# Attention's work in an extra buffer and half the ring, the first gate weights loaded and rounded during it, both layers written out

## The chip, the cores and the metric

The kernel runs on one core of a Trainium2 chip. Its engines are TensorE (PE, matrix products; PEld is its loading of weights), VectorE (DVE), ScalarE (ACT), GpSimd (POOL) and SyncE (SP), whose queue issues nearly all transfers between the chip's memory (DRAM) and the on-chip memory (SBUF). Products land in PSUM (`ps`, 8 banks of 512 floats per partition). The metric is the device time of one execution, in microseconds.

## The reference, cut to what matters

Two layers of one block, and then a second block that the change touches only in how one buffer is handed over. Of each of the two layers this matters (512 tokens, width 1024, fp32):

```python
def _mixer(h, w_in, qn_g, kn_g, w_pa, w_pb, w_o, cos, sin, slopes):
    proj = h @ w_in
    qa, ka, va, qd, kd, vd, gates = jnp.split(proj, IN_SPLITS, axis=-1)
    ...
    out_a = _global_gqa(qa, ka, va)                  # 8 heads, 2 key heads
    ...                                              # 12 dilated heads in 3 groups
    out_b = jnp.sum(wts[..., None] * jnp.stack(outs, 0), 0).reshape(b, s, B_OUT)
    g_a, g_b = jnp.split(jax.nn.sigmoid(gates), 2, axis=-1)
    merged = g_a * (out_a @ w_pa) + g_b * (out_b @ w_pb)
    return merged @ w_o
```

Behind the mixer each layer has a layer norm, a mixture of 16 experts and a second layer norm. `mod = silu(c) @ w_ada + b_ada` gives shifts, scales and gates for the norms.

## The kernel before, in words

**Products in three parts.** Every fp32 weight is cut into a rounded high part (`w_hi`) and a low part (`w_lo`), and so are the activations (`hT_hi`, `hT_lo`). A product is high*high + high*low + low*high. Raw weights arrive in `ring`, two halves of 128 x 2048 floats (1 MB each). For half `i` of unit `u`: SyncE loads `ring[i]` (L121, once the low part before is done), ScalarE rounds it into `w_hi[i]` (L132), VectorE subtracts to get `w_lo[i]` (L144), and TensorE multiplies (L283), first everything that needs `w_hi`, then what needs `w_lo`. The class `Weights` holds the semaphores.

**Stages.** A layer is a row of stages, each a block of five instruction streams with a barrier of all engines behind it: `norm_to_hT`, `in_projection`, `attention`, `branches`, `norm_to_hT`, `moe`, `norm_to_hT`. The two layers run in a hardware loop (L2495), so each engine has a jump back behind layer 1, and addresses that depend on the layer are computed in registers.

**attention** (L1570). 48 groups: 32 "global" ones (one head, 128 queries, 512 keys), then 16 "dilated" ones. For group `i`, TensorE multiplies queries and keys (L1618), VectorE takes the maximum (L1712), ScalarE the exponential into `pr` (L1670), TensorE transposes it (L1641), ScalarE (odd global groups and all dilated ones, L1691) or VectorE (even global ones, L1752) copies the result out of PSUM into `pT`, TensorE multiplies it with the values (L84), and VectorE scales the result (L1740). In each round `i` ScalarE does the exponential of group `i`, then the copy of group `i-1` if it is its own. Three buffers `pr`, three `sc` and two `pT` (512 floats each) take turns; before, all eight lie in the ring, which nothing else uses in this stage. Beside it SyncE issues, in this order and each line waiting for the one before: the two bias tables and 11.8 MB of zeros into a table in DRAM that the experts use later (`slots_x`); `v0c` out to DRAM; `v0` back in another order (three transfers). All of that is L1605, and L1611 is the last wait.

**branches** (L1758). Its first four units are the gate weights (TensorE's half units of 32 + 16 products), then the two branches and the output. SyncE: both halves of unit 0, `U0` out to DRAM (L1808), the modulation sums (`tmp_b`, `braw`, `gates`, rows), then `U0` back in another order (L1814), three pieces of `w_ada` (L1034), the halves of unit 1, more pieces. TensorE: 32 small products (`warm_up`, L102), half unit (0, 0), then the sums over rows (L1096, L1101, L1868), a wait for the modulation (`tail.mod_done`), then half unit (0, 1) and all others. VectorE: the low parts of both halves, a wait for `U0`, the weights of the three groups (L1933 to L1936), four quarter pieces (L1048, L1054), the end of the modulation (`tail.finish`, L1117), which TensorE waits for.

`k.ahead` are two semaphores, one for each half of the ring, that count loads issued in the stage before the one that uses them; they are never cleared, so the waits name totals (16 a load).

## Time and profile before

| | us |
|---|---|
| median of 3 runs | 3522.6 (3502.38 to 3526.61) |
| profiled execution | 3511.61 |
| its span in the profile | 3509.8 |
| PE busy | 3075.4 (88%) |
| DVE busy | 2230.2 (64%) |
| ACT busy | 1220.9 (35%) |
| POOL busy | 391.8 (11%) |
| attention, layer 1 and 2 | from 214.3 and from 1059.0, some 97 us each |
| branches, layer 1 and 2 | from 312.3 and from 1156.9 |

The page shows the engines' busy time, but an average over 3.5 ms says little of two places of some 100 us. The timeline (each instruction or run of equal ones with its start, its duration, and in brackets the idle time ahead of it and what ended that) is read around these places, the windows give the granted TensorE clock and the DMA engines' share in a stretch, and the waits say what a queue waited for. `SPq` are instructions of SyncE's queue.

### The profile page before, as it was taken

What the parts mean: (1) busy time and instruction counts of PE and PEld (TensorE: products, weight loads), DVE (VectorE), ACT (ScalarE), POOL (GpSimd) and SP (SyncE); (2) the same over time, 40 slices, a digit from 0 to 9 for tenths busy, and PEclk for the clock granted to TensorE, in tenths of its full rate; (3) what the DMA queues carried; (4) which work ended last, traced back from release to release, by engine and by line L of the source; (5) the groups of instructions that cost most, each with busy time, mean ns of one, the idle gap of its engine ahead of it and who ended that gap; (6) DMA issues with size and microseconds to landing.
All of it is one profiled execution on the core that took longest, in us unless ns stands there. A gap on an engine that the chain in (4) does not pass through costs nothing. (4 is left out here: it accounts for less than half of the span.)

```text
span 3509.8 us, 39676 instructions
## 1 busy us (share of the span) xinstructions
PE 3075.4 (88%) x14763; PEld 2487.9 (71%) x14763; DVE 2230.2 (64%) x3130; ACT 1220.9 (35%) x1629; POOL 391.8 (11%) x152
## 2 busy tenths in 40 slices
PE   4998977996799896899499799789999898889999
PEld 3777866774677784877377578668887687758887
DVE  6765575997666567699643747666664565464445
ACT  2234223764325333466222725431111222341112
POOL 0000001000000000100000000304443000014443
PEclk9999987998899997899699999989999899989999
DMA  7754535997645642799552033124442352112222
GB/s 249 250 177 151 192 103 182 367 403 274 221 162 175 208 159 86 275 403 395 196 191 84 25 125 100 41 83 156 143 144 69 128 174 97 60 48 95 93 93 80
DMA packets 285298, 583.87 MB, mean 166 GB/s; under 512 B 21562, under 2 KB 129538, under 8 KB 278077
## 3 DMA queue, kind: packets, MB, share of 16 engines
q1 hardware_dynamic: 272744, 537.87, 44.3%
q10 hardware_dynamic: 7764, 26.85, 1.9%
q0 software_dynamic: 4608, 16.78, 1.3%
q8 instruction: 109, 1.79, 0.2%
q14 instruction: 73, 0.59, 0.1%
HBM read 529.46 MB, written 78.71 MB: 173 GB/s over the span
## 5 line engine op out<-in xcount | busy, mean ns | idle before, releaser
L132 ACT CAST w_hi<-ring 128x2048 fp32r<-128x2048 f32 (+2 forms) x166 | 308.8, 1863 | 1212.5 <-PE ps L283 1021.8
L283 PE MATMUL ps<-hT_hi,w_hi 128*128 128x512 f32 (+1 forms) x1256 | 503.3, 401 | 25.2 <-DVEq L1117 11.3
L283 PE MATMUL ps<-hT_lo,w_hi 128*128 128x512 f32 (+1 forms) x1256 | 500.5, 399 | 0.0
L139 POOL TENSOR_TENSOR w_lo<-ring,w_hi 128x2048 fp32r<-128x2048 f32 x64 | 307.3, 4803 | 906.6 <-ACTq L2931 521.3
L144 DVE TENSOR_TENSOR w_lo<-ring,w_hi 128x2048 fp32r<-128x2048 f32 (+3 forms) x112 | 245.4, 2195 | 229.4 <-ACT w_hi L132 229.1
L283 PE MATMUL ps<-hT_hi,w_lo 128*128 128x512 f32 (+1 forms) x1256 | 307.9, 397 | 9.9 <-DVE w_lo L144 9.9
L283 PEld LDWEIGHTS ps<-hT_hi,w_hi 128*128 128x128 f32 (+1 forms) x1256 | 240.1, 191 | 86.1 <-DVEq L1117 13.0
L283 PEld LDWEIGHTS ps<-hT_hi,w_lo 128*128 128x128 f32 (+1 forms) x1256 | 237.8, 190 | 67.5 <-DVE w_lo L144 11.6
L283 PEld LDWEIGHTS ps<-hT_lo,w_hi 128*128 128x128 f32 (+1 forms) x1256 | 239.9, 191 | 56.0
L1054 DVE SCALAR_TENSOR_TENSOR piece_sums<-pieces,cond,piece_sums 128x512 f32<-128x512 f32 x294 | 220.8, 751 | 92.6 <-DMA pieces<-in_w_ada_dram 57.8
L283 PE MATMUL ps<-w_hi,hT_hi 128*128 128x512 f32 (+1 forms) x672 | 259.9, 389 | 1.0 <-ACT w_hi L132 1.0
L283 PE MATMUL ps<-w_hi,hT_lo 128*128 128x512 f32 (+1 forms) x672 | 259.0, 387 | 0.0
L283 PE MATMUL ps<-w_hi,hid_hi 128*128 128x512 f32 x448 | 174.4, 389 | 0.0
L283 PE MATMUL ps<-w_hi,hid_lo 128*128 128x512 f32 x448 | 174.4, 389 | 0.0
L2996 DVE TENSOR_TENSOR hid_exact<-hid_exact 128x512 f32<-128x512 f32 x64 | 162.1, 2532 | 4.0 <-DVE hid_exact L2993 0.6
L283 PE MATMUL ps<-w_lo,hT_hi 128*128 128x512 f32 (+1 forms) x672 | 158.2, 387 | 0.0
L283 PEld LDWEIGHTS ps<-w_hi,hT_hi 128*128 128x128 f32 x672 | 126.4, 188 | 28.6 <-issue 1.8
L283 PEld LDWEIGHTS ps<-w_hi,hT_lo 128*128 128x128 f32 x672 | 126.4, 188 | 26.8
L283 PEld LDWEIGHTS ps<-w_lo,hT_hi 128*128 128x128 f32 x672 | 124.2, 188 | 27.4 <-DVE w_lo L144 0.3
L102 PE MATMUL ps<-ident_sb 128*128 128x128 f32 x696 | 100.9, 317 | 48.6 <-PEq L72 48.6
L102 PEld LDWEIGHTS ps<-ident_sb 128*128 128x128 f32 x696 | 98.7, 231 | 51.9 <-issue 51.9
L3015 DVE TENSOR_TENSOR y<-y,ps 128x512 f32<-128x512 f32 x48 | 33.0, 688 | 157.1 <-PE ps L283 155.8
(596 smaller groups left out, 5929.6 us busy)
## 6 DMA issues: line engine op xcount, KB each, us to landing
ring<-in_mlp_w_dram SPq DMA_DIRECT2D x64, 1024.0 KB, 5.2
pieces<-in_w_ada_dram SPq DMA_DIRECT2D x96, 512.0 KB, 5.9
ring<-in_w_in_dram SPq DMA_DIRECT2D x36, 1024.0 KB, 6.5
pieces<-in_mod_w_dram SPq DMA_DIRECT2D x72, 512.0 KB, 5.1
raw_sep<-in_w_exp_gate_dram SPq DMA_DIRECT2D x50, 512.0 KB
raw_sep<-in_w_exp_up_dram SPq DMA_DIRECT2D x50, 512.0 KB
raw_sep<-in_w_exp_down_dram SPq DMA_DIRECT2D x24, 1024.0 KB
ring<-in_e_w_in_dram SPq DMA_DIRECT2D x24, 1024.0 KB, 5.6
```

What stands on the lines that cost most here:

```text
L102: pe.matmul(k.ps[:, bank, 0:P], k.ident[:], k.ident[:], start=True, stop=True)
L132: self.k.nc.scalar.copy(self.k.parts[0][:, i, 0:words], self.k.ring[:, i, 0:words]).then_inc(self.high, 1)
L139: self.k.nc.gpsimd.tensor_tensor(self.k.parts[1][:, i, 0:words], self.k.ring[:, i, 0:words], self.k.parts[0][:, i, 0:words].bitcast(F32), ...
L144: self.k.nc.vector.tensor_tensor(self.k.parts[1][:, i, 0:words], self.k.ring[:, i, 0:words], self.k.parts[0][:, i, 0:words].bitcast(F32), ...
L283: mm = pe.matmul(out, a if weight_left else b, b if weight_left else a, start=first and part == 0 and q == ks[0] and o == 0, stop=last and ...
L1054: ins = V.scalar_tensor_tensor(acc, slot[:, q, :], f, acc, ALU.mult, ALU.add)
L2996: link(V.tensor_tensor(e, e, e, ALU.mult))
L3015: link(V.tensor_tensor(yv, yv, k.ps[:, 4 * b + t, :], ALU.add))
```

## The change

- In the first block attention's eight buffers are split: `pr` and one `pT` lie in half 1 of the ring, `sc` and the other `pT` in a new buffer `work` (128 x 2048 floats). Half 0 of the ring is free.
- SyncE, behind the last of its loads in attention, loads the first half of the first gate weights into `ring[0]`.
- ScalarE, in round 24 of 48, between the exponential of group 24 and the copy of group 23, waits for that load and rounds it into `w_hi[0]`.
- In `branches` SyncE loads only half 1 of unit 0, ScalarE rounds only half 1, and TensorE's 32 warm-up products are gone.
- The loop over the layers is a Python loop: both layers are written out, and the totals of `k.ahead` become constants.
- The window attention of the second block gets its eight buffers as two fours of the same buffer.

```diff
-def attention(k, groups, loads=(), space=None, late=(), ahead=None, warm=12):
+def attention(k, groups, loads=(), space=None, late=(), ahead=None, warm=12, round_at=None):
...
-        idle = k.ring[:].rearrange("p b n -> p (b n)").rearrange("p (a n) -> p a n", a=8) if space is None else space
-        pr, sc, pT = idle[:, 0:3], idle[:, 3:6], idle[:, 6:8]
+        pr, sc, pT = space[0][:, 0:3], space[1][:, 0:3], (space[0][:, 3], space[1][:, 3])
...
             if ahead is not None:
                 k.load_ahead(sp, ahead)
+                if len(ahead) == 1:
+                    sp.nop().then_inc(k.ahead[1], 16)
...
             for i in range(N + 1):
                 if i < N:
                     soften(i)
+                if round_at is not None and i == N // 2:
+                    act.wait_ge(k.ahead[0], round_at)
+                    nc.scalar.copy(k.parts[0][:, 0, :], k.ring[:, 0, :])
                 v = i - 1
...
-            weights(0, 0)
+            sp.wait_ge(k.ahead[0], ahead)
+            sp.nop().then_inc(W.landed[0], 16)
             weights(0, 1)
...
-            split(0, 0)
+            act.nop().then_inc(W.high, 1)
             split(0, 1)
...
         def _(pe):
-            W.start_read(pe)
+            pe.nop().then_inc(W.read, 2)
+
...
+                    work = b.enter_context(nc.sbuf_tensor(fresh("work"), [P, 4, 512], F32))
...
+                              space=(k.ring[:, 1, :].rearrange("p (a n) -> p a n", a=4), work[:]),
+                              ahead=k.first_halves(kp(A["w_in"]), C_GATE, feature=True)[0:1], round_at=32 * l + 32)
...
-    with k.nc.Fori(0, DEPTH) as l:
+    for l in range(DEPTH):
         first_layer(k, l, mid)
```

ScalarE's stream in attention, at rounds 23 to 26. `L1670` before is `L1671` after, `L1691` is `L1695`; `ring` and `work` are where the buffers lie. Before:

```order
L1670 ACTIVATE ring,ls<-ps,neg_max 128x512 x2
L1691 COPY ring<-ps 128x512
L1670 ACTIVATE ring,ls<-ps,neg_max 128x512 x2
L1691 COPY ring<-ps 128x512
L1670 ACTIVATE ring,ls<-ps,neg_max 128x512 x2
```

After:

```order
L1671 ACTIVATE ring,ls<-ps,neg_max 128x512 x2
L1689 CAST w_hi<-ring 128x2048
L1695 COPY work<-ps 128x512
L1671 ACTIVATE ring,ls<-ps,neg_max 128x512 x2
L1695 COPY work<-ps 128x512
L1671 ACTIVATE ring,ls<-ps,neg_max 128x512 x2
```

The cast stands between the second exponential of a pair (group 24) and the copy of group 23.

SyncE's stream from the attention of a layer into `branches` (a branch instruction opens each stage). Before:

```order
L1605 DMA slots_x<-const_zeros_dram 128x23x1024
L1605 DMA scratch<-v0c 128x1040
L1605 DMA v_40<-scratch 128x3x260
L1605 DMA v_40<-scratch 64x260 x2
L68 UNCONDITIONAL_BRANCH
L1793 UNCONDITIONAL_BRANCH
L121 ISA
L121 DMA ring<-in_w_in_dram 128x8x256
L121 ISA
L121 DMA ring<-in_w_in_dram 128x8x256
L1808 DMA scratch<-U_98 128x4x264
```

After:

```order
L1604 DMA slots_x<-const_zeros_dram 128x23x1024
L1604 DMA scratch<-v0c 128x1040
L1604 DMA v_40<-scratch 128x3x260
L1604 DMA v_40<-scratch 64x260 x2
L264 DMA ring<-in_w_in_dram 128x8x256
L68 UNCONDITIONAL_BRANCH
L1797 UNCONDITIONAL_BRANCH
L121 DMA ring<-in_w_in_dram 128x8x256
L1813 DMA scratch<-U_98 128x4x264
```

One of the two ring loads has moved from the head of `branches` to the end of attention's list, and the register arithmetic (`ISA`) ahead of the loads is gone.

## Rows read from the trace of the kernel before

**Rows 1.** The page's first part: busy time, share of the span, instructions.
```profile
PE 3075.4 (88%) x14763; PEld 2487.9 (71%) x14763; DVE 2230.2 (64%) x3130; ACT 1220.9 (35%) x1629; POOL 391.8 (11%) x152
```

**Rows 2.** Timeline, ScalarE, attention, both layers: start, duration, what [idle before, releaser].
```profile
261.99 0.69 ACT L1670 ACTIVATE ring<-ps,neg_max 128x512 f32<-128x512 f32 x1 [0.69 <-DVE neg_max L1712]
...
263.80 0.59 ACT L1691 COPY ring<-ps 128x512 f32<-128x512 f32 x1 [1.03 <-PE ps L1641]
...
265.75 0.69 ACT L1670 ACTIVATE ring<-ps,neg_max 128x512 f32<-128x512 f32 x1 [0.69 <-DVE neg_max L1712]
...
1108.51 0.59 ACT L1691 COPY ring<-ps 128x512 f32<-128x512 f32 x1 [1.03 <-PE ps L1641]
```

**Rows 3.** Timeline, SyncE's queue, attention of layer 1.
```profile
215.19 0.71 SPq L1605 DMA_DIRECT2D slots_x<-const_zeros_dram  x1
...
265.56 1.57 SPq L1605 DMA_DIRECT2D v<-scratch  x3
```

**Rows 4.** Waits of SyncE's queue, attention of layer 1: total, times, longest.
```profile
SPq L1605 <- DMA slots_x<-const_zeros_dram: 47.0, 1, 47.0
```

**Rows 5.** Line L1611: duration in ns, first and last start (layers 1 and 2).
```profile
L1611 SPq EVENT_SEMAPHORE  x2: 17/17/17, 270.9 to 1115.5; - x2
```

**Rows 6.** Timeline, TensorE, start of branches in layer 1.
```profile
312.31 5.44 PE L102 MATMUL ps<-ident_sb 128*128 128x128 f32 x32 [1.61 <-PEq L72]
319.98 0.79 PE L283 MATMUL ps<-hT_hi,w_hi 128*128 128x512 f32 x1 [2.23 <-ACT w_hi L132]
...
340.74 1.02 PE L1868 MATMUL ps<-gates,ones_b 128*128 128x512 f32 x2
347.34 0.80 PE L283 MATMUL ps<-hT_hi,w_hi 128*128 128x512 f32 x1 [5.58 <-DVEq L1117]
```

**Rows 7.** Timeline, VectorE, the same stretch.
```profile
332.69 0.18 DVE L1933 TENSOR_TENSOR Mx<-U,U 128x16 f32<-128x16 f32 x1 [6.29 <-DMA U<-scratch]
...
345.19 1.54 DVE L1054 SCALAR_TENSOR_TENSOR piece_sums<-pieces,cond,piece_sums 128x512 f32<-128x512 f32 x2 [6.58 <-DMA pieces<-in_w_ada_dram]
```

**Rows 8.** Windows: stretch, length, busy by engine (count), PEclk, DMA share, GB/s.
```profile
314.00:333.00 19.00, 16.77 (x74) 13.95 (x73) 4.86 (x4) 3.80 (x2) 0.00 (x0) 0.85 1.01 369
323.40:341.80 18.40, 18.36 (x82) 13.05 (x80) 7.29 (x12) 1.63 (x2) 0.00 (x0) 0.91 1.05 384
347.30:350.70 3.40, 3.36 (x8) 2.68 (x9) 3.32 (x3) 0.00 (x0) 0.00 (x0) 0.52 0.49 154
400.00:440.00 40.00, 40.00 (x190) 33.45 (x189) 20.38 (x26) 11.35 (x16) 0.00 (x0) 1.00 0.52 169
279.00:310.50 31.50, 30.56 (x279) 27.94 (x278) 24.63 (x49) 20.07 (x41) 7.34 (x7) 1.00 0.01 1
3051.50:3061.70 10.20, 10.12 (x64) 8.86 (x64) 6.52 (x21) 5.84 (x22) 0.00 (x0) 0.71 0.01 2
```

**Rows 9.** Timeline, VectorE, first instruction behind layer 1 and behind layer 2.
```profile
888.38 0.69 DVE L1215 BATCH_NORM_STATS2 stats<-x_res 128x6 f32<-128x512 f32 x1 [4.99 <-issue]
...
1733.71 0.06 DVE L1105 MEMSET ones_m<- 128x1 f32 x1 [1.24 <-PEq L72]
```

**Rows 10.** Line L1670 up to 262.8 and up to 1107.5: count, ns, first and last start.
```profile
L1670 ACT ACTIVATE ring<-ps,neg_max x25: 682/690/696, 219.1 to 262.0; 128x512 f32<-128x512 f32 x25
...
L1670 ACT ACTIVATE ring<-ps,neg_max x25: 680/689/696, 1063.8 to 1106.7; 128x512 f32<-128x512 f32 x25
```

**Rows 11.** Gate load issued at 364.50 in branches: us from issue to landing.
```profile
DMA to landing us min/median/max: 5.1/5.1/5.1
```

**Rows 12.** Timeline, ScalarE, the first rounding in branches of layer 1.
```profile
318.02 1.90 ACT L132 CAST w_hi<-ring 128x2048 fp32r<-128x2048 f32 x1 [8.52 <-DMA ring<-in_w_in_dram]
```

**Rows 13.** Timeline, TensorE, window attention of the second block.
```profile
3051.58 2.08 PE L1618 MATMUL ps<-skT,sqT 64*128 64x256 f32 x8 [1.06 <-ACT attention_space L1680]
...
3058.07 1.14 PE L1618 MATMUL ps<-skT,sqT 64*128 64x256 f32 x8
...
3062.62 1.13 PE L1618 MATMUL ps<-skT,sqT 64*128 64x256 f32 x8 [0.70 <-ACT attention_space L1680]
```

More of the change, by code:

```diff
@@ L249, in __init__ @@
         self.ahead = [c.enter_context(nc.semaphore(n)) for n in ("ahead0_landed", "ahead1_landed")]
-        self.ahead_n = 16 * DEPTH
+        self.ahead_n = 32 * DEPTH
         self.bias_moved = c.enter_context(nc.semaphore("bias_moved"))
@@ L1357, in _, with in_projection @@
                         router.logits(pe, out, q)
-def in_projection(k, w, hT, T, gq, gk, w_side, side_out, ahead):
+def in_projection(k, w, hT, T, gq, gk, w_side, side_out, ahead, x_moves):
     nc = k.nc
@@ L1408, in _ @@
             sp.wait_ge(in_landed, 48)
-            sp.wait_ge(k.x_moved, 4 * ahead)
+            sp.wait_ge(k.x_moved, x_moves)
             side.end(sp, 8)
@@ L1651, in _ @@
                         n, w = vs[0].shape[-1], width(v)
-                        mm = chain(pe, k.ps[:, 4 + v % 2, h * n:(h + 1) * n], lambda j: pT[:, v % 2, h * w + j * P:h * w + (j + 1) * P],
+                        mm = chain(pe, k.ps[:, 4 + v % 2, h * n:(h + 1) * n], lambda j: pT[v % 2][:, h * w + j * P:h * w + (j + 1) * P],
                                    lambda j: vs[j], range(len(vs)))
@@ L1690, in _ @@
                         act.wait_ge(o_ready, v - 1)
-                    nc.scalar.copy(pT[:, v % 2], k.ps[:, 2 + v % 2, :]).then_inc(t_act, 1)
+                    nc.scalar.copy(pT[v % 2], k.ps[:, 2 + v % 2, :]).then_inc(t_act, 1)
         @block.gpsimd
@@ L1751, in _ @@
                         dve.wait_ge(o_ready, v - 1)
-                    V.tensor_copy(pT[:, v % 2], k.ps[:, 2 + v % 2, :]).then_inc(t_dve, 1)
+                    V.tensor_copy(pT[v % 2], k.ps[:, 2 + v % 2, :]).then_inc(t_dve, 1)
                 if i >= 2:
@@ L1755, in _, with branches @@
             dve.wait_ge(o_out, N)
-def branches(k, w_in, wa, wb, wo, hT, T, tail_of, sums, b, g1, g2, w_side):
+def branches(k, w_in, wa, wb, wo, hT, T, tail_of, sums, b, g1, g2, ahead, w_side):
     nc = k.nc
@@ L2427, in first_layer @@
                 in_projection(k, kp(A["w_in"]), hT, T, A["q_norm_g"][l], A["k_norm_g"][l],
-                              lambda s: ada[0][:, :, 2 * D + s * WIDE:2 * D + (s + 1) * WIDE], lambda s: sums[:, s * WIDE:(s + 1) * WIDE], 16 * l + 16)
+                              lambda s: ada[0][:, :, 2 * D + s * WIDE:2 * D + (s + 1) * WIDE], lambda s: sums[:, s * WIDE:(s + 1) * WIDE], 32 * l + 16, 64 * l + 64)
                 T["oa"] = T["qa"]
@@ L2435, in first_layer @@
                               loads=[[(band[:], k.K["bias_band"]), (cls[:], k.K["bias_class"]),
-                                      (k.slots_x.rearrange("(b p) d -> p b d", p=P), bcast(k.K["zeros"], 1, BLOCKS))]] + order_v0(k, T["v0c"], T["v0"]))
+                                      (k.slots_x.rearrange("(b p) d -> p b d", p=P), bcast(k.K["zeros"], 1, BLOCKS))]] + order_v0(k, T["v0c"], T["v0"]),
+                              space=(k.ring[:, 1, :].rearrange("p (a n) -> p a n", a=4), work[:]),
+                              ahead=k.first_halves(kp(A["w_in"]), C_GATE, feature=True)[0:1], round_at=32 * l + 32)
             first = k.sums_2[0].rearrange("p (l n) -> l p n", l=2)[l]
@@ L2441, in first_layer @@
             branches(k, kp(A["w_in"]), kp(A["w_branch_a"]), kp(A["w_branch_b"]), kp(A["w_out"]), hT, T,
-                     (sums[:, D:3 * D], A["b_ada"][l][3 * D:5 * D], 16, k.mod[:, 24:40], (8,), None), sums, A["b_ada"][l][2 * D:6 * D], g1, g2,
+                     (sums[:, D:3 * D], A["b_ada"][l][3 * D:5 * D], 16, k.mod[:, 24:40], (8,), None), sums, A["b_ada"][l][2 * D:6 * D], g1, g2, 32 * l + 32,
                      (lambda s: 0 if s < n_next else 1, lambda s: at(ada[1], s) if s < n_next else at(w_first, s - n_next),
@@ L3660, in odd_mixer @@
             ring = lambda i: k.ring[:, i, :].rearrange("p (k n) -> p k n", k=4)
-            attention(k, groups, warm=28, space=space, late=moves, ahead=[(ring(i), wo[:, KD:KD + 4, 512 * i:512 * (i + 1)]) for i in range(2)])
+            attention(k, groups, warm=28, space=(space[:, 0:4], space[:, 4:8]), late=moves, ahead=[(ring(i), wo[:, KD:KD + 4, 512 * i:512 * (i + 1)]) for i in range(2)])
             hT = pair_of(nc, h, "hT", [P, KD, S], side="right")
```

## Prediction, made before the change was timed

> **What bounds the kernel now.** The page comes first: TensorE is busy for 88% of the span [rows 1], so time is won where it stands still or runs at its lower clock. The change touches three such places: the attention and the start of the stage behind it (`branches`), each once per layer, and the edge between the two layers. I read the timeline of each, engine by engine.
>
> *Attention.* The groups go round in a steady beat, two groups in 3.77 us (exponential 24 starts at 261.99 and 26 at 265.75 [rows 2]). TensorE has no idle time in it, and ScalarE has two short gaps in a beat: 1.03 us ahead of the copy of the transposed weights, which waits for TensorE's transposes, and 0.69 us ahead of every second exponential, which waits for VectorE's maximum. What matters for the change is SyncE's queue beside it [rows 3]: it issues a transfer of 11,776 KB of zeros at 215.19 and waits 47.0 us for it [rows 4]; the reordering of `v0` then takes two dependent steps more (the second is issued at 265.56), and the last wait ends at 270.9 in layer 1 and at 1115.5 in layer 2 [rows 5].
>
> *Start of `branches`.* The first product is at 319.98, though TensorE entered the stage at 312.31: it waits for the load and the rounding of half 0 [rows 6]. Half 0 and the sums behind it end at 341.76 (340.74 plus 1.02). Then TensorE stands still for 5.58 us, and the second half unit starts at 347.34. What ends last there is not a weight but VectorE, which must first work on four quarter pieces and finish the modulation sums. Its own waits end on transfers: `U` at 332.69 and the fourth piece at 345.19 [rows 7]. From 314 to 333 the DMA engines' share is 1.01, and from 323.4 to 341.8 it is 1.05 [rows 8]. So the second half unit, behind which TensorE is busy nearly all the time (40.00 of 40 us from 400 to 440 [rows 8]), is held by the bytes queued on SyncE's queue. Layer 2 looks the same.
>
> *Edge of the layers.* VectorE's first instruction of layer 2 starts at 888.38, after 4.99 us of idle time that nothing but issue explains. At the end of layer 2, out of the same stage but with no jump back, it is 1.24 us [rows 9].
>
> **The change part by part.**
>
> 1. *The wait inside attention.* ScalarE's new rounding stands behind exponential 24 and ahead of the copy for group 23, as the order shows. It waits for the load of the first gate half, which SyncE issues behind everything of [rows 3 to 5]. Exponential 24 is the 25th of its kind: 25 have started by 262.0 and by 1106.7 [rows 10]. Layer 1: the issue at 270.95; landing after 5.1 us, as the same form of load took on a quiet queue [rows 11], with 0.1 for the slower of the others in that stage, so 5.2; landed 276.15. The rounding is 1.90 us (the same cast at 318.02 [rows 12]): done 278.05. The copy that it pushes stood at 263.80, so 14.25 us late. Layer 2: 1115.55 + 5.2 + 1.90 = 1122.65 against 1108.51 [rows 2], 14.14 us late. Queued behind the waiting instruction on ScalarE are all later exponentials and copies; TensorE needs the copy for its next value product and exponential 25 for its next transposes, VectorE needs those products for its results. Nothing else feeds them, so all stop within a beat. Work done meanwhile is one maximum and one copy on VectorE; at the restart that saves the 0.69 us wait, once. Sum: 28.4 - 1.4 = +27.0 us.
>
> 2. *TensorE's clock after that stop.* TensorE stands still for about 13 us. After the 5.58 us stop at 341.8 the granted clock was 0.52 for the next 3.4 us [rows 8], the lower of the two levels (1.2 GHz). What an attention beat costs there is shown by the window attention of the second block: from 3051.58 to 3058.07, most of it at the low clock (mean 0.71 from 3051.5 to 3061.7 [rows 8]), a pair of groups took 6.49 us, and 4.55 us from there to 3062.62 at the full one [rows 13]. That is 1.9 us for a pair. Bounds: nothing, and two such pairs, 3.9 us. I take one, 1.9 us a layer: +3.8 us.
>
> 3. *The 1 MB load leaves `branches`.* SyncE's list there loses its first transfer and keeps its order. TensorE then starts products at once, some 7.6 us earlier (319.98 - 312.31), and the half unit and its sums are done some 7 us earlier. But the next half unit waits for the modulation, and that for the fourth piece. Its bytes stand in one queue with one load fewer: 1.05 MB at 384 GB/s (the row for 323.4 to 341.8 [rows 8]) is 2.7 us. The removed issue lies in this time. Bounds: nothing if latency and not bytes sets the chain; 7.6 us if the pieces are no bound. A share of 1 is that of a full queue, so 2.7 us: -5.4 us for both layers.
>
> 4. *The 32 warm-up products go.* They lay ahead of the first product and end with it; in that half unit even a cold start is hidden, since TensorE has over ten microseconds to wait behind it. Eight products at 0.43 us (3.40 us for 8 [rows 8]) in place of 0.21 (40 us for 190) would cost 1.8 us there and reach nobody. If that cover were gone it would be 1.8 us a layer. Nothing.
>
> 5. *Both layers written out.* The jump back goes: 4.99 - 1.24 = 3.75 us. SyncE loses register arithmetic ahead of its issues; in both stages above it waits for others or for bytes, so I count nothing for that. Sum: -3.75 us.
>
> 6. *The extra buffer and half the ring* have the same shapes and the same rotation of three and two, so no wait is added. Nothing. The window attention gets the same space cut in two: nothing.
>
> Sum: 27.0 + 3.8 - 5.4 - 3.75 = **+21.7 us**. On the profiled execution, 3511.6 us with a span of 3509.8, that is 3533 us. The median of the runs shown, 3522.6, would give 3544. The profiled one lies between the runs (3502.38 to 3526.61), so I say 3538 us. Between -35 and +35 us lies what a measurement of this kernel cannot tell from no change (1%), and my forecast is inside it.
>
> **The rivals.**
>
> *B: the start of `branches` is worth all of the 7.6 us.* For it: TensorE's idle time ahead of the first product names ScalarE's rounding. Against it: the 5.58 us stop behind it. Time: 27.0 + 3.8 - 15.2 - 3.75 = +11.9, so 3528 us.
>
> *C, the other side: ScalarE does not stop.* Were the first gate half there by 262.8, the rounding would fill the 1.03 us gap and cost 0.87 us more a layer, and the sum is 1.7 - 5.4 - 3.75 = -7.4, so 3509 us. That needs the zeros' transfer to be some 13.4 us shorter than its 47.0 us, or the wait not to hold. It decides where the copy comes 4.6 us late in each layer, half of the gains' 9.15 us. Against it: SyncE's last wait ends 8.9 us behind exponential 24 in layer 1 and 8.8 us in layer 2 [rows 5, 10], so the place is steady, and nothing that the change moves stands ahead of it.
>
> *D: the clock stays low for the rest of attention.* From 279 to 310.5 TensorE is busy for 30.56 of 31.50 us at clock 1.00 [rows 8], so at half clock it would need up to twice that: up to +30 us a layer, 3538 + 56 = 3594 us at the most, and 3566 us if half of the stretch is low. Against it: the window attention came back to 1.00 after two pairs [rows 13].
> The Trainium skill has a rule for D: "TensorE: Matmul & The Clock Gate", section "HAM oscillation — how this bites in real kernels", says that small gaps between groups of products can let the clock swing between its levels. The trace of attention does not agree: 1.00 through the whole stage. By the rule the sum would be D's, by the row it is mine.
>
> **How the numbers follow.** Forecast 0.72, B 0.12, C 0.05, D 0.11. The range takes in B and the runs' own scatter below, and half of D's lower case above: 3510 to 3566 us. Faster by over 1% needs a case that I don't have: 0.02. Slower by over 1% is D and the upper end of the forecast (second pair at the low clock, a median like the 3526 run): 0.18. The rest, 0.80, lies within 1%.
>
> **What would show it.** Right: in each layer a single ScalarE idle time of about 13.5 us ahead of the new cast, ended by the load of the ring; SyncE's last wait in attention still near 271; attention longer by 15 to 17 us; the first product of `branches` right at the stage's entry, but the second half unit only some 2.7 us earlier in its stage; VectorE's gap between the layers 1.2 us. Wrong: the cast starts within 2 us of exponential 24 (C); the second half unit follows the first without a stop (B); the granted clock at 0.5 for over 10 us behind the restart (D).

## The result and the profile after

The changed kernel takes 3525.3 us (median of 22 runs, 3517.9 to 3538.7), the kernel before beside it 3518.5 us (22 runs): ratio 1.0023, 95% interval 1.0012 to 1.0034, that is 8 us more (4 to 12). I had said 21.7 us more. The time lies in my range and within the 1%, but the change of the time was forecast nearly three times too large, and it will show that this came from errors of opposite sign, of which the largest is in step 5.

Three places carry the result. First ScalarE and SyncE in attention of both layers (timeline: start, duration, what, idle before and who ended it; the SPq rows are SyncE's issues), to be held against [rows 2, 3]:

```profile
261.31 0.69 ACT L1671 ACTIVATE ring<-ps,neg_max 128x512 f32<-128x512 f32 x1 [0.69 <-DVE neg_max L1716]
...
271.62 1.90 ACT L1689 CAST w_hi<-ring 128x2048 fp32r<-128x2048 f32 x1 [9.53 <-DMA ring<-in_w_in_dram]
273.42 0.58 ACT L1695 COPY work<-ps 128x512 f32<-128x512 f32 x1
...
1121.24 0.69 ACT L1671 ACTIVATE ring<-ps,neg_max 128x512 f32<-128x512 f32 x1 [0.69 <-DVE neg_max L1716]
...
1132.91 1.90 ACT L1689 CAST w_hi<-ring 128x2048 fp32r<-128x2048 f32 x1 [10.89 <-DMA ring<-in_w_in_dram]
1134.72 0.58 ACT L1695 COPY work<-ps 128x512 f32<-128x512 f32 x1
```

```profile
262.68 1.56 SPq L1604 DMA_DIRECT2D v<-scratch  x3
266.48 0.39 SPq L264 DMA_DIRECT2D ring<-in_w_in_dram  x1
```

Exponential 24 starts at 261.31, and the cast waits 9.53 us in layer 1 and 10.89 us in layer 2 for the load of the ring, just the one idle time that the prediction named, though 4.0 and 2.6 us shorter than its 13.5 us. The copy used to follow the exponential by 1.81 us (263.80 against 261.99 [rows 2]); now it follows by 12.11 and by 13.48, so it is 10.3 and 11.7 us late.

TensorE behind the stop of layer 1, as timeline and as windows (length, busy time of each engine, granted clock, DMA share, GB/s), the last three windows those of layer 2:

```profile
263.76 0.61 PE L1642 MATMUL ps<-ident_sb,ring 128*128 128x128 f32 x4
274.05 1.97 PE L84 MATMUL ps<-kva,work 128*128 128x64 f32 x8 [9.68 <-ACT work L1695]
275.95 2.08 PE L1619 MATMUL ps<-kaT,qaT 64*128 64x512 f32 x4
...
283.06 2.08 PE L1619 MATMUL ps<-kaT,qaT 64*128 64x512 f32 x4
```

```profile
274.00:301.60 27.60, 27.55 (x124) 23.02 (x125) 10.49 (x26) 8.46 (x21) 2.10 (x2) 0.50 0.00 1
303.00:312.40 9.40, 9.33 (x93) 8.38 (x93) 8.49 (x18) 5.89 (x12) 2.10 (x2) 1.00 0.00 1
312.40:331.00 18.60, 18.45 (x165) 16.96 (x164) 13.84 (x27) 12.21 (x25) 4.20 (x4) 1.00 0.00 1
1135.30:1141.50 6.20, 6.15 (x24) 4.53 (x25) 1.05 (x3) 2.44 (x7) 0.00 (x0) 0.52 0.00 0
1141.50:1149.00 7.50, 7.50 (x69) 6.49 (x69) 5.19 (x14) 3.51 (x11) 0.00 (x0) 1.00 0.00 0
1149.00:1172.00 23.00, 22.12 (x207) 19.93 (x206) 19.35 (x40) 13.28 (x29) 6.29 (x6) 1.00 0.01 2
```

In layer 1 of this execution the granted clock is 0.50 (the level of 1.2 GHz) when TensorE goes on, a beat takes 7.11 us (from 275.95 to 283.06) in place of 3.77, and the clock is back only at some 301.6, after 27.6 us in which TensorE was busy for 27.55 us and did half of what it does at the full clock. In layer 2 it is back after some 6 us, though the stop ahead of it was longer. The first of these is what the prediction gave as a sign of rival D: 0.5 for over 10 us behind the restart.

Start of `branches` in layer 1, TensorE and then VectorE, against [rows 6, 7]:

```profile
333.32 0.47 PE L283 MATMUL ps<-hT_hi,w_hi 128*128 128x512 f32 x1 [1.47 <-ACTq L1839]
333.63 0.39 PE L283 MATMUL ps<-hT_lo,w_hi 128*128 128x512 f32 x1
333.86 0.40 PE L283 MATMUL ps<-hT_hi,w_hi 128*128 128x512 f32 x1
...
363.65 0.80 PE L283 MATMUL ps<-hT_hi,w_hi 128*128 128x512 f32 x1 [9.46 <-DVEq L1117]
```

```profile
350.05 0.19 DVE L1939 TENSOR_TENSOR Mx<-U,U 128x16 f32<-128x16 f32 x1 [6.20 <-DMA U<-scratch]
...
361.50 1.54 DVE L1054 SCALAR_TENSOR_TENSOR piece_sums<-pieces,cond,piece_sums 128x512 f32<-128x512 f32 x2 [5.52 <-DMA pieces<-in_w_ada_dram]
```

Products begin at the stage's entry. The stop ahead of the second half unit is still there, for the same pieces, and grew from 5.58 to 9.46 us. That half unit starts 30.3 us behind the entry (363.65 - 333.32) in place of 35.0 (347.34 - 312.31 [rows 6]), and the pieces still end what VectorE waits for.

The edge of the layers, against 4.99 in [rows 9]:

```profile
903.98 0.69 DVE L1215 BATCH_NORM_STATS2 stats<-x_res 128x6 f32<-128x512 f32 x1 [1.02 <-PEq L72]
```

The page's first part, against [rows 1], names no bound that moved: the products are fewer by the 64 warm-ups, and the time longer.

```profile
span 3532.6 us, 38936 instructions
...
PE 3079.9 (87%) x14699; PEld 2489.7 (70%) x14699; DVE 2231.5 (63%) x3130; ACT 1217.6 (34%) x1628; POOL 391.3 (11%) x152
```

### The profile page after: what moved, and what is told of

The parts are those of the page before. It is cut to its first block and busy times, and to the rows that moved or that the text cites. A ratio compares the mean times of both kernels' runs of the same rounds, so it can differ in the third digit from the quotient of the medians.

```text
span 3532.6 us, 38936 instructions
## 1 busy us (share of the span) xinstructions
PE 3079.9 (87%) x14699; PEld 2489.7 (70%) x14699; DVE 2231.5 (63%) x3130; ACT 1217.6 (34%) x1628; POOL 391.3 (11%) x152
## 5 line engine op out<-in xcount | busy, mean ns | idle before, releaser
L283 PEld LDWEIGHTS ps<-hT_hi,w_lo 128*128 128x128 f32 (+1 forms) x1256 | 235.8, 188 | 65.8 <-DVE w_lo L144 10.7
```

The lines of the kernel that those rows point to most:

```text
L283: mm = pe.matmul(out, a if weight_left else b, b if weight_left else a, start=first and part == 0 and q == ks[0] and o == 0, stop=last and ...
```

## The experiments

A table first. Medians; "clock" is the mean granted clock over all runs of a kernel (the kernel before: 0.9284 over 88 runs). Ratios are to runs of the kernel before on the same chip in the same job, whose medians were 3518.9 (the first four rows), 3514.6 (buffers split and 72 calls), 3516.6 (the next four), 3519.7 (4 writes) and 3518.2 (1 and 8 writes).

| kernel | us (runs) | ratio, 95% interval | clock |
|---|---|---|---|
| the change again | 3526.5 (12) | 1.0038 [1.0017, 1.0059] | 0.9254 |
| only written out | 3497.1 (6) | 0.9938 [0.9923, 0.9954] | 0.9327 |
| change, load issued first | 3495.5 (6) | 0.9940 [0.9926, 0.9955] | 0.9317 |
| change, rounding in round 32 | 3505.2 (5) | 0.9958 [0.9946, 0.9971] | 0.9294 |
| written out, buffers split | 3493.5 (6) | 0.9932 [0.9916, 0.9948] | 0.9323 |
| change, 72 warm-up calls in the stop | 3530.5 (10) | 1.0039 [1.0022, 1.0056] | 0.9326 |
| two loops of one pass | 3496.5 (8) | 0.994 [0.9922, 0.9959] | 0.9336 |
| change with the loop | 3539.7 (5) | 1.0067 [1.0039, 1.0095] | 0.9242 |
| change, 40 warm-up calls in the stop | 3527.1 (10) | 1.0036 [1.0016, 1.0056] | 0.9286 |
| change, load first and round 32 | 3499.0 (10) | 0.9962 [0.9945, 0.998] | 0.9295 |
| two loops, 4 writes between | 3510.3 (10) | 0.9977 [0.9962, 0.9992] | 0.9308 |
| two loops, 1 write between | 3502.1 (10) | 0.9955 [0.9937, 0.9973] | 0.9327 |
| two loops, 8 writes between | 3515.1 (10) | 0.9992 [0.9977, 1.0007] | 0.9307 |

**The change again.**

> The changed kernel once more, beside the others of this job. The runs gave a ratio of 1.0023 to the kernel before, and the single profiled execution was 22.8 us longer in span. Theory A (the stop of ScalarE costs about 10.4 us a layer, the start of branches gives back 4.4, the edge of the layers 4, TensorE's clock adds an amount that differs from execution to execution): ratio 1.002 to 1.004. Rival (the profiled pair is typical): 1.006.

Measured: the casts start at 270.27 and 1115.61, behind 8.55 and 10.39 us of idle time, and the low clock behind the stop of layer 1 is over sooner: the beats are back at 3.77 us from 279.62 on. The long stretch at the low clock is thus no fixed cost, but it is one that comes. The three profiles with a stop (these two and that of the change with the loop, below) hold six stops of TensorE, of 8.7 to 11.0 us. Read by the transposes behind them (four take 1.1 us at the low clock and 0.6 us at the full one), the low clock lasted some 28, 6, 4, 6, 13 and 6 us, and the longest stretch did not follow the longest stop.

**Only the writing out.** The kernel before with `for l in range(DEPTH)` in place of the loop over the layers.

> The kernel before with both layers written out and nothing else. The edge of the layers should lose its 4.99 us of issue time for about 1.1 us. Theory A: -4 us, ratio 0.9989, and both attentions as before (98 us each). Rival (writing out does nothing, or costs elsewhere in fetching code): ratio 1.000 or above.

Measured: 0.9938, some 22 us less where the theory had 4 and the rival none. This is the surprise of the case: at the edge only 4 us are gained.

**The stop taken away in two ways.** The load issued ahead of the bias tables and the zeros:

```diff
             n = 0
+            if ahead is not None and loads:
+                k.load_ahead(sp, ahead)
+                sp.nop().then_inc(k.ahead[1], 16)
             for pairs in loads:
```

> The changed kernel, but SyncE issues the ring's load ahead of the bias tables and the zeros in attention, so that it has landed long before round 24. Theory A: ScalarE doesn't stop, the new rounding costs up to 0.9 us a layer, attention is 98 to 100 us long, and against the kernel before the time is -4 (edge) - 9 (branches) + 2 = -11 us, ratio 0.997. Rival 1 (the stop is not what costs, but the split buffers or the rounding itself are): ratio stays at 1.002. Rival 2 (TensorE's clock falls in attention for another reason): attention stays above 105 us.

and the wait with its rounding put to the first dilated group (32), which waits for SyncE's loads anyway:

```diff
             for i in range(N + 1):
-                if i < N:
-                    soften(i)
-                if round_at is not None and i == N // 2:
+                if round_at is not None and i == first_bias:
                     act.wait_ge(k.ahead[0], round_at)
                     nc.scalar.copy(k.parts[0][:, 0, :], k.ring[:, 0, :])
+                if i < N:
+                    soften(i)
```

> The changed kernel, but the wait and the rounding stand at the head of round 32, ahead of the first dilated exponential, where ScalarE waited 2.53 us for GpSimd in the kernel before. The load lands 10.3 us behind exponential 24 in the changed kernel, round 32 is 14 us behind it. Theory A: no stop, the rounding lies in the gap, attention 98 us, ratio 0.9965 (-12 us). Rival (the rounding pushes the first dilated groups by its 1.9 us): -8 us, 0.9977.

Measured: 0.9940 and 0.9958. The timeline of ScalarE in the first of them:

```profile
258.89 0.19 ACT L1672 ACTIVATION_READ_ACCUMULATOR ring<-ps,neg_max 128x1 f32 x1
258.99 1.89 ACT L1690 CAST w_hi<-ring 128x2048 fp32r<-128x2048 f32 x1
260.77 0.58 ACT L1696 COPY work<-ps 128x512 f32<-128x512 f32 x1
```

The same cast in the same round with nothing to wait for: 31 us less than the change (3526.5 - 3495.5, same job). So the stop, with all that it brings behind it, costs the change about 31 us, give or take some 10 by the intervals of the two ratios, and my +27.0 and +3.8 were 30.8.

**The kernel before, two further profiles.**

> The kernel before, profiled once more. Its profiled execution of 3511.6 us is 7 us under the median of 22 runs, and writing out the loop alone brought 22 us where the edge of the layers shows 4. Theory A (the rest is a place that is slow in most executions with the loop, but not in the profiled one): a stage whose length differs by 5 us or more from the profile that I have. Rival (scatter spread over all stages by TensorE's clock): no stage differs by more than 3 us.

> The kernel before, a third profile, for the same question: under theory A the same stage is long again, under the rival other stages are.

Measured: 3501.7 and 3521.9 us, clocks 0.934 and 0.929. One kernel's profiles are 20 us apart, so stages are compared below as means over several.

**Written out, buffers split, nothing else.**

> The kernel before with both layers written out and attention's buffers split between half 1 of the ring and the new buffer; no load or rounding in attention, and branches as before. My step 6 says that the split costs nothing: ratio 0.994, as with the writing out alone. Rival (the place of the buffers matters): off by more than 0.002.

Measured: 0.9932 against 0.9938 without the split: the buffers cost nothing, as step 6 said.

**Keeping TensorE busy in the stop.** First 72 calls of the warm-up product, then 40:

```diff
                     v = i - 2
+                    if round_at is not None and v == N // 2 - 1:
+                        pe.wait_ge(o_out, v - 1)
+                        warm_up(k, pe, 4 + v % 2, 72)
                     moved_out(pe, v)
```

> The changed kernel with 72 small products on TensorE in the stop (about 8.6 us at the full clock), so that its clock does not fall while ScalarE waits. They lie behind the last product that it can do and end before the copy that it waits for. Theory: a stop of 10.4 us a layer stays, what the clock costs behind it (12.8 and 3.5 us in the two layers of the profile) goes: 10 to 15 us faster than the changed kernel, ratio 0.999. Rival (the clock costs little in most executions): ratio 1.003 as the changed kernel.

> The changed kernel with 40 calls of the warm-up product (80 products as the profile counts them, at 0.113 us each some 9.0 us) while TensorE stands still in attention, about 9.7 us in each layer. They end ahead of the stop's end, so that the stop is no longer than in the change; the 72 calls of the experiment before took 16.2 us and made it 5.6 us longer. Theory A, the low clock behind the stop costs a good part: the granted clock is 1.00 behind the stop, attention is 3 to 10 us a layer shorter than in the change, 3510 to 3520 us, ratio 0.998 to 1.001. Theory B, the clock costs my 1.9 us a layer: 3522 us. If the stop of itself were the smaller part, attention plus projection would fall from 259 to 269 us to under 255.

The timeline of TensorE with 72 calls (a call stands as two products), then with 40, and a window behind each:

```profile
261.11 16.24 PE L102 MATMUL ps<-ident_sb 128*128 128x128 f32 x144
277.19 1.00 PE L84 MATMUL ps<-kva,work 128*128 128x64 f32 x8
```

```profile
277.00:312.00 35.00, 34.12 (x309) 29.97 (x307) 26.27 (x58) 18.36 (x40) 6.29 (x6) 1.00 0.00 1
```

```profile
263.09 9.10 PE L102 MATMUL ps<-ident_sb 128*128 128x128 f32 x80
272.02 1.00 PE L84 MATMUL ps<-kva,work 128*128 128x64 f32 x8
272.96 1.13 PE L1619 MATMUL ps<-kaT,qaT 64*128 64x512 f32 x4
...
276.73 1.13 PE L1619 MATMUL ps<-kaT,qaT 64*128 64x512 f32 x4
```

```profile
280.00:287.00 7.00, 7.00 (x68) 6.32 (x67) 5.69 (x14) 2.96 (x7) 1.05 (x1) 1.00 0.01 2
287.00:312.00 25.00, 24.13 (x225) 21.81 (x223) 20.42 (x41) 14.84 (x32) 7.33 (x7) 1.00 0.01 2
```

With 72 calls the products outran the stop, which ScalarE would have ended at 272.2 (its copy starts at 271.63), so that experiment doesn't separate the two costs; it shows only that the clock is 1.00 for the rest of attention when TensorE hadn't stood still. With 40 calls the stop has nearly its own length (in layer 1 they end about 1 us later than ScalarE's copy would have let TensorE go on), and the beat is 3.77 us at once (272.96 to 276.73). Projection plus attention is 255.4 and 257.0 us in the two layers; what the two parts cost follows with the profiles of the kernels with and without a stop (table below). But the timed runs don't follow that profile, which is one of the two quickest of ten (3506 and 3508, the other eight 3520 to 3538): the median is no less than that of the change, 3527.1. That theory A's stage came true and its total did not stays open.

**Is it the jump or the register?** The kernel before with one loop of one pass for each layer:

```diff
-    with k.nc.Fori(0, DEPTH) as l:
-        first_layer(k, l, mid)
+    for at in range(DEPTH):
+        with k.nc.Fori(at, at + 1) as l:
+            first_layer(k, l, mid)
```

> The kernel before, with its one loop over the two layers made two loops of one pass each. Every engine still works out its addresses from the layer's register, but no engine jumps back between the layers, and each layer has its own instructions. Writing out both layers gave 0.9938 [0.9923, 0.9954], some -21.8 us, of which only 4 us stood at the edge. Theory A, the gain comes from the jump back and the instructions behind it being fetched anew: 3497 +- 4 us, ratio 0.994, the edge 18.9 us in place of 22.9. Theory B, it comes from the layer's register (arithmetic and waits ahead of transfers and instructions, all through both layers): ratio 0.999, -4 us, all at the edge. A share in between is told by the stages of the two layers.

Measured: 0.994, all of the gain. But the kernel is not what the expectation says. The first lines of the pages of the kernel before, of the two loops and of the kernel only written out:

```profile
span 3509.8 us, 39676 instructions
```

```profile
span 3492.5 us, 39092 instructions
```

```profile
span 3502.7 us, 39062 instructions
```

With loops of one pass nearly all the work on addresses (FUSED_REGOPS and MOVE, instructions on registers) is gone as well. At L121 the kernel before has these, and the two loops have neither:

```profile
L121 SPq FUSED_REGOPS  x64: 37/37/56, 70.0 to 1321.9; - x64
L121 SPq MOVE ring<-in_w_in_dram x40: 29/29/38, 70.1 to 1231.3; - x40
```

Over the whole trace SyncE's queue has 278 FUSED_REGOPS and 417 MOVE before, 42 and 74 with the two loops, 42 and 72 written out. So this experiment takes the jump back and the register arithmetic away together, as writing out does, and **can't tell one from the other**. It shows that the gain comes again in a second form. VectorE behind the edge:

```profile
886.28 0.17 DVE L1114 TENSOR_TENSOR mod<-ps,bcol 128x16 f32<-128x16 f32 x1
887.74 0.69 DVE L1215 BATCH_NORM_STATS2 stats<-x_res 128x6 f32<-128x512 f32 x1 [1.28 <-PEq L72]
```

1.28 us of idle time for 4.99. One more trace of the loop lies in the page's two queues of instructions: 109 and 73 packets before, 106 and 63 with the two loops and written out.

**The change with the loop put back.**

> The change without its writing out: the loop over the layers is put back into the changed kernel, all else stays. Theory A, writing out is worth some 21 us here too: 3526 + 21 = 3547 us, ratio 1.0085. Theory B, my step 5 (only the jump back): 3526 + 4 = 3530 us, ratio 1.003.

Measured: 3539.7 us, 1.0067, where 1.0023 and 1.0038 were measured written out. Here writing out is worth 10 to 16 us, between the two theories.

**Load first and round 32.**

> The changed kernel with the first gate half loaded ahead of the bias tables and zeros (issued near 213, landed long before it is wanted), and the wait and the rounding at the first group behind the dilated tables' wait. Either alone gave 0.9940 and 0.9958. If the rounding between exponential 24 and its copy costs 0.9 us a layer, as the gap of 1.03 us says, this one stands 1 to 2 us below the early load alone: 3493 us, ratio 0.9935. If the rounding costs nothing anywhere, or the load beside the zeros costs what it saves, it is the same as the early load: 3495 us.

Measured: 0.9962, not faster than either alone. The two don't add up, and no version with the load moved out of `branches` beats the ones that are only written out (0.9938, 0.9932, 0.994).

**Does it matter when the work falls?** Two loops of one pass (so without the register arithmetic) with writes of zeros by VectorE between the layers, four, then one and eight:

```diff
+        if at:
+            with k.nc.sbuf_tensor(fresh("pause"), [P, 4, 1024], F32) as pause, k.nc.Block() as block:
+                @block.vector
+                def _(dve):
+                    for _i in range(4):
+                        k.nc.vector.memset(pause[:, _i], 0.0)
```

> The two loops of one pass again, with four writes of 128x1024 zeros by VectorE between the layers (2 to 5 us with the stage around them), so that the edge is about as long as with the jump back and all work behind it begins about when it did in the kernel before. Theory A1, the jump back costs 4 us at the edge and something else all through the second layer and behind it: this kernel keeps all but those 4 us, 3496 + 4 = 3500 us, mean granted clock 0.933. Theory A2, only the time by which the rest is shifted matters to the low-clock stretches behind it: it is back near 3513 us or above, mean granted clock 0.928 to 0.929 as in the kernel before.

> Two loops of one pass with one write of zeros between the layers in place of four: the added stage is the same, the shift is about 1.7 us in place of 4.9. Four writes gave 3510.3 us, 13.8 more than none, 4.9 of them at the edge. If the 8.9 us beyond the shift come from when the work behind the edge falls (theory A2), one write costs its 1.7 us and some part between 0 and 9 us, and the mean clock says which. If they come from having any stage more there, it is 3496.5 + 1.7 + 8.9 = 3507 us, and the eight writes behind it show the same 8.9.

> The same with eight writes of zeros, a shift of about 9.2 us. Theory A2 (when the work falls): 9.2 us and anything from 0 to some 20 us, with a mean clock between 0.928 and 0.934 that goes with it. A loss of 8.9 us that any added stage brings: 3496.5 + 9.2 + 8.9 = 3514.6 us, mean clock 0.931 as with four writes.

VectorE between the layers with four writes:

```profile
886.44 0.17 DVE L1114 TENSOR_TENSOR mod<-ps,bcol 128x16 f32<-128x16 f32 x1
888.07 0.91 DVE L2501 MEMSET pause<- 128x1024 f32 x1 [1.46 <-PEq L72]
...
892.58 0.69 DVE L1215 BATCH_NORM_STATS2 stats<-x_res 128x6 f32<-128x512 f32 x1 [0.37 <-PEq L2497]
```

From the modulation's last instruction to the layer's first are 6.14 us here and 1.46 us with no write, a shift of 4.7 us. With one write it is 1.5 us and with eight 9.0 us by the same rows. Against 3496.5 us with none:

| writes | shift at the edge | longer by | beyond the shift | mean clock |
|---|---|---|---|---|
| 0 | 0 | 0 | 0 | 0.9336 |
| 1 | 1.5 | 5.6 | 4.1 | 0.9327 |
| 4 | 4.7 | 13.8 | 9.1 | 0.9308 |
| 8 | 9.0 | 18.6 | 9.6 | 0.9307 |

Four writes came out between the two theories (3510.3 us, clock 0.931). One write should have cost 3507 us if any added stage brought the 8.9 us; it has 3502.1 (ten runs, none above 3504.9). These rows come from three jobs; by the ratios to the kernel before the three are longer by 5, 13 and 18 us, each give or take some 8 us, so what one write costs beyond its shift is not clear of noise. Within one job, eight writes are 13.0 us longer than one (3515.1 - 3502.1; the ten runs of each leave 8 to 17) for 7.5 us more at the edge. So time put between the layers costs more than its own length, by the medians up to 9 us more, and the clock of the runs falls with it.

**Where does the clock go?** More profiles of the kernel before and of the two loops.

> The kernel before, one more profile. The runs of the kernel before fall around mean clocks of 0.927 and 0.933, the longer ones at 0.927; profiles so far had 0.932, 0.934 and 0.929, and the one at 0.929 had 34 us more at the low clock between 2365 and 3090 us of the second block, and was 12 us longer there. If the gain of writing out that single profiles don't show (some 10 of the 21 us) is that stretch, a profile of this kernel at 0.925 to 0.929 has it in the second block: some 788 us in place of 771 to 777 us for that part. If it is lost in the second layer, the part stays at 774 and branches and moe of layer 2 are longer than 200 and 315 us.

> The kernel before, a further profile for the same question: of the runs of this kernel about three in four lie at a mean clock of 0.929 or less, so about three in four profiles should have the 788 us part in the second block, if that is where the clock goes.

> The two loops of one pass, a second profile: all eight runs had a mean clock of 0.931 to 0.935. If the second block's part is what tells the two kernels apart, it is 774 us here and the span is 3490 to 3497 us; if it is 785 to 788 us at such a clock, the second block isn't where they differ.

Measured: 3512.5, 3511.8 and 3497.0 us at 0.931, 0.929 and 0.932. The second block's part (from VectorE's first work behind 2365 us to its first at 3146 us) is 776.7 us in both profiles of the kernel before: at 0.929 I had expected 788. That theory falls. The part from 2365 to 3090 us does come in two lengths, but in kernels of the same gain. The windows of it, first the two loops, then the kernel only written out:

```profile
2365.00:3090.00 725.00, 681.83 (x3099) 548.29 (x3099) 434.02 (x604) 173.14 (x236) 143.81 (x30) 0.96 0.36 117
```

```profile
2365.00:3090.00 725.00, 685.81 (x3066) 552.19 (x3064) 432.41 (x601) 171.85 (x234) 143.89 (x30) 0.94 0.35 115
```

Clock 0.96 against 0.94, the part 774 against 785 us, and their medians are the same.

**Stages, as means over profiles.** A stage is counted from VectorE's first instruction in it to the first in the next (the second block from its first layer norm statistics). "Before" are its five profiles, "written out" four (only written out, buffers split, two loops twice), "no stop" three (load first, round 32, both), "stop" three (the change twice, and with the loop), "40 calls" one.

| us | before | written out | no stop | stop | 40 calls |
|---|---|---|---|---|---|
| projection and attention 1 | 247.4 | 246.4 | 246.3 | 264.3 | 255.4 |
| branches 1 | 198.8 | 198.2 | 194.9 | 194.8 | 196.7 |
| moe 1 | 314.3 | 315.5 | 312.9 | 314.4 | 315.0 |
| last norm of layer 1, with the edge | 22.8 | 19.0 | 18.9 | 20.1 | 18.9 |
| projection and attention 2 | 247.5 | 246.9 | 247.3 | 259.6 | 257.0 |
| branches 2 | 199.5 | 198.5 | 197.7 | 195.8 | 197.2 |
| moe 2 | 315.7 | 312.2 | 313.5 | 313.9 | 309.4 |
| second block | 1770.3 | 1769.1 | 1767.3 | 1771.9 | 1762.2 |
| VectorE's last instruction at | 3506.5 | 3495.8 | 3489.0 | 3524.9 | 3501.0 |

## Why the prediction was wrong

**Step 1, the wait: right in kind, too long by a fifth.** ScalarE stops once in each layer behind exponential 24, for the ring's load. The copy is 10.3 and 11.7 us late, 22.0 in all, where the sum had 27.0. The landing was right: 5.14 us (266.48 to 271.62) and 5.22 us in layer 2, forecast 5.2. The issue was not. I took it at the end of SyncE's last wait, 270.9 [rows 5], 5.4 us behind the issue of the last reordering [rows 3]; it is 3.80 us behind it (262.68 to 266.48), and that reordering itself stood 1.4 us behind exponential 24 in place of 3.6. Why those transfers were done sooner no run shows.

**Step 2, the clock: right in kind, too small.** The stage with the stop is 262.0 us on the mean of both layers (264.3 and 259.6), 256.2 with TensorE kept busy, and 246.8 without a stop: 9.4 us a layer for the standing still, 5.8 us for the clock, where I had 1.9. The 256.2 is a single profile, but the low stretches agree with it: half of the six (28, 6, 4, 6, 13 and 6 us) is some 5 us a layer. Two things were too small in my 1.9 us. A beat of attention at the low clock costs 3.3 us more (7.11 - 3.77), not 1.9: the pair in [rows 13] ended at the full clock, and the one that I took off it has 0.70 us of idle time. And the low clock can last far longer than a beat. The errors of steps 1 and 2 cancel: 15.2 us a layer, forecast 15.4. Rival D's mechanism is thus real, and its sign came in two of six stops (28 and 13 us at 0.50), but not to the end of attention each time. The rows against D in the prediction came from a stretch that had had no such stop ahead of it (1.06 us of idle time in [rows 13] and 2.81 us just before), which was no fair witness.

The Trainium skill, "TensorE: Matmul & The Clock Gate", section "HAM oscillation — how this bites in real kernels", says that a wait between groups of products throws the clock back and that each such group then starts cold. (It speaks of waits longer than a group's own products. Small gaps, of which the prediction speaks, stand in the page's next section, "A second HAM failure mode: psum-queue depth-cycling".) The traces agree for the one long wait: 0.50 behind 9.68 us of idle time, and 1.00 where products filled it. That the clock stayed low for 27.6 us in which TensorE stood still for only 0.05 us is more than the section says.

**Step 3, the start of `branches`: right in its stage, absent in the total.** 3.9 us in layer 1 and 1.8 to 3.7 us in layer 2 by the table (198.8 to 194.9; 199.5 to 197.7 and 195.8), forecast 2.7 each; the second half unit comes 4.7 us earlier in its stage in layer 1. The row behind my rate, 384 GB/s, was that of a full queue, but the removed load moved at the stage's entry, where the queue was only filling. This window of the trace of before, which I had not read, gives 226 GB/s, and 1.05 MB at that is 4.6 us, an estimate:

```profile
312.30:318.00 5.70, 5.44 (x32) 5.25 (x32) 0.08 (x2) 0.00 (x0) 0.00 (x0) 0.70 0.76 226
```

Rival B falls: the stop ahead of the second half unit is there, and longer. But the kernels without a stop are not faster in timed runs than those only written out (3495.5, 3505.2, 3499.0 against 3497.1, 3493.5, 3496.5), and their mean clock is lower (0.930 against 0.933). The 4 us by which `branches` is shorter than in those (198.2 to 194.9, 198.5 to 197.7) are not in the medians, which scatter by as much; where they go was not found.

**Step 4, the warm-ups: right.** The first half unit runs at a product each 0.23 us from the start (333.63 to 333.86), with nothing cold to hide, since TensorE comes out of attention at clock 1.00.

**Step 5, writing out both layers: this step failed.** I read the edge, 4.99 - 1.24 = 3.75 us, priced the jump back by that alone, and put SyncE's register arithmetic at nothing because its queue waits in the two stages that I had read. The edge is right, 3.8 us in the table. The whole is 22 us (0.9938, 0.9932, 0.994), and 10 to 16 us in the changed kernel. The term was thus three to six times too small; what makes up the rest is open. What the runs showed in its place:
- The jump back and the register arithmetic are both gone in every kernel that gains, in the two loops of one pass too, and no run has one without the other. The stages speak for what lies at and behind the edge: before it, in layer 1, projection, attention, `branches` and `moe` are 760.5 us before and 760.1 us written out, in layer 2 they are 762.7 and 757.6 us. But the arithmetic stands in both layers, and single profiles of a stage differ by 2 to 6 us, so this does not settle it.
- The profiles of the two groups differ by 10.7 us (3506.5 - 3495.8): 3.8 at the edge, 3.5 in `moe` of layer 2, the rest in small pieces.
- The profiled executions are no fair sample: those of the kernel before had a mean clock of 0.931 where its 88 runs have 0.9284, the four others also 0.931 where their 21 runs have 0.9329. Among the runs of one kernel, 0.001 of mean clock goes with 2.3 us (219 runs). 0.0026 and 0.0017 are 9.9 us more, and 10.7 + 9.9 is 20.6.
- Time put in at the edge costs more than its length: 4.7 us of it 13.8 us. By that curve, an estimate, the jump's 3.7 us (5.16 less 1.46) would bring 7 or 8 us beyond themselves, 11 of the 20 us between the two loops and the kernel before in their job. That work that falls later meets the low clock more often fits with the clock of those runs; in which stage it does no profile showed.
- Some 9 us more are what is left between the kernel with four writes, whose edge is 1.0 us longer than with the jump (6.14 against 5.16), and the kernel before (0.9977, 3 to 13 us). These two differ in the jump and in the register arithmetic, and either may be the reason. Straight instructions with the arithmetic kept in would tell; they were not run.

The Trainium skill, "Runtime: NRT & Kernel Launch", section "Instruction fetch mechanics", says that a taken branch to instructions outside the fetched window makes the engine wait for a new fetch. The edge agrees with that, 4.99 against 1.28 us, and so do the 13 packets more in the queues of instructions; the section gives no reason for anything behind the edge, and no run here shows an engine waiting for instructions elsewhere.

**Step 6, the buffers: right**, 0.9932 against 0.9938.

**The sum.** Forecast 27.0 + 3.8 - 5.4 - 3.75 = +21.7. Measured: the change less the writing out is +0.86% to +1.01%, some 30 to 36 us where the other terms made 25.4, and the writing out -22 where I had -3.75. Taken in the other order, the change with the loop kept is +0.67% (0.39% to 0.95%), some 24 us, close to the 25.4, and writing out is then -10 to -16. The parts don't simply add, but in either order it is the writing out that was priced far too low. The total came out at +8. That the time fell into the range was luck: the range is wide, and the errors of steps 1 and 2 went opposite ways. Rival C, the other side, did not come: the cast waited 9.5 and 10.9 us.

## What to carry to other kernels

Before rounding or loading is moved into a tight loop, look at when its load can be issued: the same cast, in the same round, costs 31 us behind a queue that is late and nothing that can be seen where the load is issued first. A term that a profile shows at one edge can be a small part of the whole where all behind it shifts: take it away alone and time it, before it is bundled with others, since here it hid most of a loss of some 30 us behind a result of 8. When an experiment is built to keep one thing and drop another, count in its trace that the one is still there: two loops of one pass looked like the register without the jump, and had neither. And judge differences below half a per cent by medians with the mean clock beside them, not by a single profile of each kernel.

## What the hardware showed that I had not expected

- A loop of two passes over some 845 us of work each, with its addresses worked out in registers, costs 22 us, 0.6%, against straight instructions, though VectorE stands still for only 3.7 us more at the jump. As two loops of one pass, where the arithmetic and the jump are both gone, it costs nothing (3496.5 us; straight instructions 3497.1).
- 4.7 us put between two stages made the kernel 13.8 us longer, 9.0 us made it 18.6 us longer, and the mean granted clock fell from 0.9336 to 0.931.
- Behind one stop of 9.68 us the granted clock was 0.50 for 27.6 us in which TensorE was busy for 27.55 us, while in the other layer of the same execution, behind a stop of 11.04 us, it was back after some 6 us.
